# First merge tile prepared one delta-rule step earlier, one shared ScalarE table for logarithm and exponential, and the gates of tile 2 ahead of a norm

## The reference

```python
x += W_out( sig(gA) * W_pA(GatedDeltaNet_bidir(n)) + sig(gB) * W_pB(DilatedWindowAttn_ALiBi(n)) ),  n = RMSNorm(x)
x += ExpertChoiceSwiGLU(RMSNorm(x))
...
oa = rmsnorm(o_fwd + o_bwd, a_norm) * silu(z)                       # 8 heads of 64
weights = softmax(stack(lses), axis=0); ob = sum(weights * stack(outs))
return einsum('bsd,de->bse', gate_a * ya + gate_b * yb, w_out)
...
aff = softmax(xt @ w_router); gate, idx = top_k(aff.T, cap)         # 16 experts
```

## Time and profile before

| | us |
|---|---|
| median of 3 runs (lowest to highest) | 2291.83 (2286.57 to 2296.42) |
| the profiled execution: its own time / its span | 2283.24 / 2281.6 |
| busy: PE, DVE, ACT, POOL | 2156.3, 1315.6, 978.7, 548.8 |
| delta rule, merge, experts (rough starts in the span) | 983, 1159, 1488 |
| mean granted clock of TensorE | 0.977 |

### The profile page before, as it was taken

One profiled execution on the slowest core, in us unless ns is written; L12 is line 12 of the kernel. 1 busy time (PEld: TensorE's weight loads), 2 busy tenths in 40 slices (PEclk: granted clock), 3 DMA queues, 4 the chain that ended last, 5 costly groups with the idle time before them and its releaser, 6 DMA issues. The chain is left out here.

```text
span 2281.6 us, 41960 instructions
## 1 busy us (share of the span) xinstructions
PE 2156.3 (95%) x17318; PEld 1686.0 (74%) x17318; DVE 1315.6 (58%) x1541; ACT 978.7 (43%) x1353; POOL 548.8 (24%) x562
## 2 busy tenths in 40 slices
PE   6999999999999999888888999989999999999995
PEld 5777788899999997677744555567777777777774
DVE  5555411125575648745555448866666666666665
ACT  4666611011111108712264553255565566555654
POOL 1000000002578646833332220001111112111110
PEclk9999999999999999998889999989999999999998
DMA  3233432229888858879854441448888788877887
GB/s 132 65 100 102 111 130 105 79 89 248 225 231 228 209 160 269 259 194 241 249 194 137 134 132 55 185 175 299 292 301 300 279 290 304 307 283 281 294 288 279
DMA packets 269487, 469.79 MB, mean 206 GB/s; under 512 B 152272, under 2 KB 194896, under 8 KB 242192
## 3 DMA queue, kind: packets, MB, share of 16 engines
q1 hardware_dynamic: 187760, 396.02, 51.9%
q0 software_dynamic: 15296, 48.32, 7.4%
q10 hardware_dynamic: 66272, 23.21, 4.3%
HBM read 363.90 MB, written 107.49 MB: 207 GB/s over the span
## 5 line engine op out<-in xcount | busy, mean ns | idle before, releaser
L78 DVE TENSOR_TENSOR ex_w_rest<-weights,ex_w_rounded 128x2048 fp32r<-128x2048 f32 x192 | 434.6, 2291 | 199.4 <-ACT ex_w_rounded L2814 199.4
L2814 ACT CAST ex_w_rounded<-weights 128x2048 fp32r<-128x2048 f32 x192 | 360.1, 1908 | 89.1 <-PE ex_p_acc L2739 76.7
L2723 PE MATMUL ex_s_acc<-ex_w_rounded,ex_xt 128*128 128x512 f32 x1024 | 298.5, 400 | 0.9 <-DVE ex_xpt L2908 0.9
L2723 PEld LDWEIGHTS ex_s_acc<-ex_w_rounded,ex_xt 128*128 128x128 f32 x1024 | 187.0, 189 | 62.0 <-issue 27.2
L2723 PE MATMUL ex_s_acc<-ex_w_rest,ex_xt 128*128 128x512 f32 x512 | 159.3, 392 | 0.0
L2677 POOL DMA_INDIRECT ex_xs<-hn,rt_sample_idx x16 | 16.0, 998 | 586.9 <-PE ex_s_acc L2761 479.1
L85 PE MATMUL ch_wide<-normed,ch_w_rounded 128*128 128x512 f32 x384 | 154.2, 402 | 2.8 <-PEq L48 2.2
L85 PE MATMUL ch_wide<-normed_rest,ch_w_rounded 128*128 128x512 f32 x384 | 152.5, 397 | 0.0
L85 PE MATMUL ch_wide<-normed,ch_w_rest 128*128 128x512 f32 x384 | 152.5, 397 | 0.0
L2723 PE MATMUL ex_y_acc<-ex_w_rounded,ex_ht 128*128 128x512 f32 x512 | 150.0, 400 | 0.0
L2169 PE MATMUL mg_out<-weights,mg_mix_t 128*128 128x512 f32 x288 | 129.0, 601 | 2.5 <-ACT mg_mix_t L2293 2.5
(11 more groups left out here) (410 smaller groups left out, 4435.7 us busy)
## 6 DMA issues: line engine op xcount, KB each, us to landing
weights<-in_w_expert SPq DMA_DIRECT2D x192, 1024.0 KB, 7.0
tk_w<-in_w_tok SPq DMA_DIRECT2D x10, 1344.0 KB, 7.4
ch_w<-in_w_ch SPq DMA_DIRECT2D x24, 512.0 KB, 5.2
sc_rows<-rows SPq DMA_DIRECT2D x40, 256.0 KB
sc_qk<-qkv_ch SPq DMA_DIRECT2D x40, 256.0 KB, 6.1
laq<-sc_laq ACTq DMA_DIRECT2D x80, 128.0 KB, 3.4
dl_kv<-qkv_tok SPq DMA_DIRECT2D x40, 256.0 KB, 3.9
dl_kq<-laq SPq DMA_DIRECT2D x20, 512.0 KB, 5.0
```

Of the source, the lines that this page charges most:

```text
L78: return dve.tensor_tensor(out, whole, rounded.bitcast(F32), ALU.subtract)
L2723: mm = pe.matmul(banks[:, b], x[:, k, x_part], w[:, i % SPLIT, kk, 512 * b:512 * b + 512], start=(k == 0 and x_part == 0 and w is w_hi), s ...
L2814: act.copy(w_hi[:, i % SPLIT], raw(i)).then_inc(w_rounded, 1)
```

## The change

Nothing computed changes but the following. In the delta rule the first tile's Silu moves from ahead of the last step's `dl_v` copy to behind that copy in step 18 (the last but one), `roots` moves to the end of step 18 and DVE's `statistics` behind step 18's `carried`; `weighted` comes straight after the last `remainder`. The last step's `to_state`, `keep` and `carried`, whose state nobody reads, are left out. The Sigmoid of tile 0's gates moves out of the delta block to behind ScalarE's first copy in the merge. ScalarE loads one table set that holds both logarithm and exponential by an explicit instruction behind every Silu and Sigmoid pair, so that the two functions need no loads of their own. The copy `mix_out(0)` moves ahead of tile 1's logarithm. On DVE `gated(2, 0)` moves ahead of `normed(0)`, and at the end of the merge `normed(8)` stands behind one round of ranking instead of two after the residual, and `residual(9, 1)` behind one round of the high tiles less. A one-element Ln, which only loaded a table, goes.

```diff
@@ -1732,7 +1732,7 @@
                     solve(s, b)
                     if more:
                         correction(s + 1, nb)
-                    to_state(s, b)
+                        to_state(s, b)
                     to_output(s, b)
                 idle_bank = uobank[:, 1, 0].rearrange("p h c -> p (h c)")[:, 0:P]
                 keep_busy(pe, idle_bank, ident, 4)
@@ -1746,12 +1746,10 @@
             @block.scalar
             def _(act):
                 def step(s, b, i, prompt):
-                    if isinstance(s, int) and s == STEPS - 1:
-                        first_tile.activate(act)
                     act.wait_ge(v_done, s + 1)
                     act.copy(paired(vb[:]), vbank).then_inc(v_out, 1)
-                    if isinstance(s, int) and s == STEPS - 1:
-                        first_tile.roots(act)
+                    if isinstance(s, int) and s == STEPS - 2:
+                        first_tile.activate(act)
                     act.wait_ge(at_done, s + 1)
                     if not early(s, 2):
                         act.wait_ge(stored[b % 2], 32 * (2 * i + b // 2))
@@ -1767,8 +1765,9 @@
                         load_inverse(act, dr, x1[nb], loaded[nb], s + AHEAD_STEPS)
                     for d, chunk in enumerate(places(s, prompt)):
                         act.dma_start(dr["o_delta"][d, bass.ds(chunk * CH, CH), :], ostage[HD * (1 - d):HD * (1 - d) + HD, b % 2].rearrange("p h c -> p (h c)")).then_inc(stored[b % 2], 16)
+                    if isinstance(s, int) and s == STEPS - 2:
+                        first_tile.roots(act)
                 ring_steps(act, step)
-                first_tile.open_gates(act)
 
             @block.vector
             def _(dve):
@@ -1810,18 +1809,18 @@
                     more = not (isinstance(s, int) and s == STEPS - 1)
                     nb = (b + 1) % RING
                     remainder(s, b)
-                    if more:
-                        masked(s + 1, nb)
+                    if not more:
+                        first_tile.weighted(dve)
+                        return
+                    masked(s + 1, nb)
                     keep(s, b)
-                    if more:
-                        transposed(s + 1, nb)
-                    else:
+                    transposed(s + 1, nb)
+                    carried(s, b)
+                    if isinstance(s, int) and s == STEPS - 2:
                         first_tile.statistics(dve)
-                    carried(s, b)
                 masked(0, 0)
                 transposed(0, 0)
                 ring_steps(dve, step)
-                first_tile.weighted(dve)
 
 
 def delta_constants():
@@ -1871,6 +1870,9 @@
 GANGS = EXPERTS // GANG
 QUARTERS = P // CAP_P
 QUARTER = D // QUARTERS
+LN_AND_EXP = "natural_log_exp_and_others"
+
+
 class FirstTile:
 
 
@@ -1926,6 +1928,7 @@
         act.activation(self.z, self.z, ACT.Silu).then_inc(self.silu, 1)
 
     def roots(self, act):
+        act.preload_act_table_set(LN_AND_EXP)
         act.wait_ge(self.mean, 1)
         act.wait_ge(self.eps_set, 1)
         act.activation(self.st[:, 8:16], self.st[:, 8:16], ACT.Ln, bias=self.eps[:], scale=1.0 / HD).then_inc(self.ln, 1)
@@ -1939,13 +1942,14 @@
 
     def statistics(self, dve):
         st, m = self.st, self.att[:, :, GH * HD:GH * HD + GH]
-        dve.wait_ge(self.squared, 1)
-        dve.tensor_reduce(st[:, 8:16], self.sq.rearrange("p (h c) -> p h c", h=HEADS), AX.X, ALU.add).then_inc(self.mean, 1)
+        dve.wait_ge(self.loaded, 16 * self.LOADS)
         dve.tensor_tensor(st[:, 28:32], m[:, 0, :], m[:, 1, :], ALU.max).then_inc(self.dm, 1)
         dve.wait_ge(self.dm, 1)
         dve.tensor_tensor(st[:, 28:32], st[:, 28:32], m[:, 2, :], ALU.max).then_inc(self.dm, 1)
         dve.wait_ge(self.dm, 2)
         dve.tensor_tensor(st[:, 16:28].rearrange("p (g h) -> p g h", g=3), m, st[:, 28:32].unsqueeze(1).to_broadcast([P, 3, GH]), ALU.subtract).then_inc(self.dm, 1)
+        dve.wait_ge(self.squared, 1)
+        dve.tensor_reduce(st[:, 8:16], self.sq.rearrange("p (h c) -> p h c", h=HEADS), AX.X, ALU.add).then_inc(self.mean, 1)
 
     def weighted(self, dve):
         st, done = self.st, self.weighted_done
@@ -2304,6 +2307,7 @@
 
                 last_sample = NT + 2
                 turned_out(0)
+                first_tile.open_gates(act)
                 for c in range(1, NT + LAST):
                     if has(c - 4):
                         t, b = c - 4, c % 2
@@ -2325,6 +2329,9 @@
                         act.activation(z[:, b], z[:, b], ACT.Silu).then_inc(S["silu"], 1)
                         if c >= 2:
                             open_gates(c)
+                        act.preload_act_table_set(LN_AND_EXP)
+                        if c == 1:
+                            mix_out(0)
                         act.wait_ge(S["sumsq"], c + 1)
                         act.activation(st[b][:, 8:16], st[b][:, 8:16], ACT.Ln, bias=eps[:], scale=1.0 / HD).then_inc(S["ln_on"], 1)
                         act.wait_ge(S["ln_on"], c + 1)
@@ -2332,16 +2339,14 @@
                         act.wait_ge(S["dm"], c + 1)
                         act.activation(st[b][:, 16:28], st[b][:, 16:28], ACT.Exp).then_inc(S["eatt"], 1)
                     if c == 1:
-                        mix_out(0)
                         open_gates(1)
+                        act.preload_act_table_set(LN_AND_EXP)
                     if has(c - 4):
                         act.wait_ge(S["hn_turned"], c - 3)
                         act.copy(hn_t[:], wide_turned[:]).then_inc(S["hn_t"], 1)
                     if c == last_sample - 1:
                         exponentials(c - 4)
                         mix_out(c - 2)
-                    if c == last_sample:
-                        act.activation(unused[:], eps[:], ACT.Ln).then_inc(S["ln_ready"], 1)
                     if has(c - 1) and c >= 2:
                         turned_out(c - 1)
 
@@ -2357,7 +2362,9 @@
 
                 def gated(t, h):
                     b, cols, n = t % 2, slice(h * 512, h * 512 + 512), 2 * t + h + 1
-                    if h == 0:
+                    if h == 0 and t == 0:
+                        dve.wait_ge(first_tile.gate_done, 1)
+                    elif h == 0:
                         dve.wait_ge(S["sig"], t + 1)
                         if t >= 2:
                             dve.wait_ge(S["mix_turned"], t - 1)
@@ -2478,11 +2485,13 @@
                     if has(c - 5):
                         highest(c - 5)
                     low_best(low_n)
+                    if c == 4:
+                        gated(c - 2, 0)
                     if has(c - 4):
                         normed(c - 4)
                     if has(c - 5):
                         affinities(c - 5)
-                    if has(c - 2) and c > 2:
+                    if has(c - 2) and c > 2 and c != 4:
                         gated(c - 2, 0)
                     if has(c):
                         statistics(c)
@@ -2516,11 +2525,12 @@
                 residual(NT - 2, 0)
                 high_best(3)
                 residual(NT - 2, 1)
+                high_best(1)
+                normed(NT - 2)
                 high_best(2)
-                normed(NT - 2)
                 residual(NT - 1, 0)
                 low_best(ROUNDS - low_rounds[0])
-                high_best(4)
+                high_best(3)
                 residual(NT - 1, 1)
                 high_best(1)
                 highest(NT - 2)
```

More of the change, by code:

```diff
@@ L2050, in phase_merge @@
             "sig", "on_turned", "on_t", "y_done", "ga", "gb", "mixed", "mix_turned", "mix_t", "out_done", "x2", "sqx", "ln_x", "rstd_x", "hn", "hn_turned", "hn_t",
-            "logits", "lmax", "lneg", "lexp", "lrec", "aff", "aff_turned", "aff_taken", "ranked", "low_ranked", "merge", "prompt_listed", "quartered", "listed", "const", "filled", "ln_ready")}
+            "logits", "lmax", "lneg", "lexp", "lrec", "aff", "aff_turned", "aff_taken", "ranked", "low_ranked", "merge", "prompt_listed", "quartered", "listed", "const", "filled")}
         inputs = [sem(f"mg_inputs{b}") for b in range(2)]
```

1 line of the change is left out of this document (removed).

## The result

| | before | after |
|---|---|---|
| median, us (lowest to highest, runs) | 2292.99 (2286.57 to 2297.13, 6) | 2275.09 (2271.04 to 2281.11, 6) |
| profiled execution, own time / span | 2283.24 / 2281.6 | 2271.04 / 2269.4 |
| busy: PE, DVE, ACT, POOL | 2156.3, 1315.6, 978.7, 548.8 | 2155.1, 1314.4, 941.3, 547.8 |
| mean granted clock of TensorE | 0.977 | 0.972 |

The ratio is 0.9924, 95% interval 0.9911 to 0.9937: 17.9 us by the medians, 14 to 20 by the interval. The prediction was 2277.7, faster.

The account below looks back on a forecast made before the run. TensorE was taken to bound the kernel, with gains only in its gaps: 2.7 + 1.4 + 5.5 + 3.0 + 1.5 = 14.1 us off the median 2291.83, giving 2277.7 us, range 2268 to 2289.

Parts of the forecast that it names:

- Barrier: End of the delta rule: barrier moves from 1158.33 to 1155.6, the last output's store ending last; 2.7 us gained.
- the lower bound's case: Barrier behind the delta rule: gain 0 if TensorE's idle multiplications run at half clock, 7.7 us, reaching 1158.9.
- the upper bound of 3.3: Same barrier: 3.3 us if the last product is through a whole 1.9 us earlier and the rest goes at once.
- `mix_out(0)`: Tile 0's mix in the merge: ScalarE's copy begins at 1177.5 instead of 1178.90, ahead of the roots; 1.4 us gained.
- 16 matmuls: Start of the merge, at 1179.94: clock may stay high behind a shorter gap, 8.62 to 7.03; 1.6 us, outside the sum.
- Fourth step: Merge, before project_in(2, 1): gates' product no longer waits for tile 0's norm, gap 7.16 falls near 1.7; 5.5 us gained.
- DVE's weighting of tile 3: DVE in the merge: 0.5 us, outside the sum, among the possible upward gains of 5.1.
- The clock there: Fourth step's next 12 matmuls: clock stays high behind the shorter gap, 8.19 to about 5.2; 3.0 us, lower bound 0.
- the first rival: Fourth step: TensorE's clock falls anyway behind the shorter gap; gain 11.1 or less, 2280.7 us; chance 0.14.
- End of the merge: Before the last tile's transposes: earlier norm closes the whole 1.50 us gap, idle multiplications then bound; 1.5 us, 1.3 if only load counts.
- Price of a load: ScalarE table loads: 1.28 us and no pause; rival of 2.66 per switch, gain about 10.5, 2281.3 us, chance 0.03.
- The sign's rival: Step 18: Silu delays output copy and next new values if loads land late; 0.05 together with all else slower.

Follow-up runs that it names:

- second profile: The changed kernel profiled once more, unchanged: stretch (last copy of new values in the delta rule to TensorE's first expert instruction) 322.94 us, against 322.77 in its first.
- ranking back: Changed kernel with normed(8) and residual(9, 1) in their old places among the ranking rounds at the merge's end: 323.71 us from delta rule's last new-values copy to experts.
- scan kept busy: Changed kernel with three idle multiplications (six instructions) ahead of the solve in each delta rule step: ratio 0.9908 to the kernel before, the 19 steps 159.26 us.
- tables alone: Kernel before with only the shared table for logarithm and exponential loaded explicitly, nothing moved: ratio 0.9963 to the kernel before.
- order alone: Kernel before with only gated(2, 0) moved ahead of normed(0) on DVE: ratio 0.9960 to the kernel before.
- second pair: Kernel before and changed kernel, both unchanged, each profiled again: 340.06 and 322.94 us from the delta rule's last new-values copy to the experts.

## Why the prediction was right

**Barrier, 2.7 predicted, 2.42 and 1.94 measured.** The store was placed rightly: 6.8 us behind the last copy in both profiles, from 1155.6 - 1148.86 = 6.7 in the prediction. But it was to be the last to end, and it was not: the idle multiplications ran partly at half clock, the lower bound's case in part, and ended 0.3 behind it (4.55 long), in the second profile 0.8 (5.11 long). Where they took 3.84, with the ranking back and with the scan kept busy, the store, 5.9 and 6.0 behind the last copy, did end last, and the first transposes came 8.03 behind that copy: the upper bound of 3.3. That the shorter gap would also leave the transposes at full clock (0.67) I had named for the projections only. Those gained nothing in the first profile, 5.40 in place of the 3.6 of full clock, and 1.92 in the second.

**`mix_out(0)`, 1.4 and 1.37.** The size is right, the mechanism only in part. The tables alone give 1.24 of it, since the load between logarithm and exponential, which the copy had stood behind, is gone; the moved copy adds 0.14. What the moved copy gives without the tables was not run; by the earlier trace rows it would pass the same load. Which of the two edits one credits is a matter of order.

**16 matmuls, left out at 1.6, 1.09 and -0.06.** That the clock stays high for them because the gap ahead shrinks from 2.48 to 1.10 is not shown: with the same gaps they took 7.13 and 8.83. What the profiles bear out is that with the shorter gaps only one of two groups at the merge's start is slow where both were; the two pieces together gain 1.01 in the first pair and 1.86 in the second. Which of the two it is stays open.

**Fourth step, 5.5 and 6.53.** The order was the mechanism. The term was too small by what the prediction had put beside the sum at 0.5: DVE's weighting of tile 3 ended 0.9 earlier. That is the tables' share: with the order alone the gap was 1.51, near the forecast's 1.7.

**The clock there, 3.0 and 2.94.** This settles the first rival: behind a gap of 1.51 (order alone) and of 0.64 (whole change) the eight matmuls took 3.70; behind 3.70 in two kernels they took 6.60 and 6.42.

**End of the merge, 1.5 and 1.67.** As predicted, the idle multiplications bound it, with no gap behind them. The load was to give 1.3 by itself, and the tables alone gave 1.08.

**Price of a load.** 1.28 in every row of all fourteen profiles, also three in a row, so the rule of 2.66 per switch cited in the prediction ("ScalarE: Activation LUTs", section "What ACT_TABLE_LOAD costs", of the Trainium skill) does not hold here.

**The sign's rival.** Silu in step 18 delayed nothing: ScalarE idled 0.73 behind it.

The terms of the sum, 14.1 predicted, measured 2.42 + 1.37 + 6.53 + 2.94 + 1.67 = 14.93, and 14.52 in the second pair; with what was left out, 16.67 and 17.12. By the medians it is 17.9, so the forecast was low by 2.6 to 3.8 us. Most of that is the clock at the start of the merge, which it had named but not added, and the 1.0 of the fourth step. The profiled execution came close, 2271.04 for 2269.1, by luck: 16.67 us gained in the stretch stood against 4.35 lost to scatter ahead of it. Judged by that one pair of spans, 12.2, one would have found a loss that no edit causes.

## What to carry to other kernels

A gap of an engine whose clock is gated can cost more than its length: 7.16 us of idle time cost another 2.9 behind it. But which group behind several short gaps runs slow differs between executions of one kernel (5.40 and 7.13 in one, 3.70 and 8.83 in the other), so two profiles and the sum over the groups are needed before a short gap gets the credit. Look for the one product in a list that stands behind a wait it does not need, and put it ahead. Before reading a gain from two profiles, cut both at the same instructions and compare piece by piece; here the scan moved by 9 to 10 us between executions of one kernel, half the gain. Two edits that shorten the same gap overlap (7.7 and 6.7 for each alone), so they are measured together and apart.

## What the runs showed of the hardware that was not expected

The granted clock of nearly the same code, the scan, was 0.83 to 0.90 over twelve executions, and six small multiplications a step in a gap of 0.92 us raised it to 0.94 and 0.98. Where it held, eight steps in a row took 7.6 us each; steps of 9.6 to 9.9 us, one to five in each of the twelve, were gone. The same edit came with three executions of 3155 to 7689 us in eleven; whether it causes them was not tried further. At the start of the merge, with a gap of 1.10 or 1.24 ahead of the 16 matmuls, the low clock fell on the projections before them in eight profiles and on those 16 in a ninth. A table load took 1.28 us wherever it stood, also behind a load of another set, and the instruction behind it started at once.
